# Hybrid decoder trunk on one core: parameters and memory weights of the S5 stage loaded inside the mixer, in shared on-chip rooms

## What is computed

```python
def s5_mixer(u, A_re, A_im, B_re, B_im, C_re, C_im, log_step, D, w_glu, b_glu):
    ug = u.reshape(b, L, 16, 16); delta = exp(log_step)[:, None]
    mag, ang = exp(A_re * delta), A_im * delta
    lr, li = mag * cos(ang), mag * sin(ang)
    ...                       # Bb = (B_re, B_im) scaled by (lambda - 1) / A
    xr, xi = scan(x[t] = lambda * x[t-1] + Bb @ ug[t])       # complex, 64 states
    y = C_re @ xr - C_im @ xi + D * u
    g = gelu(y)
    return g * sigmoid(g @ w_glu + b_glu)

def reference(x, mem, ...):
    mn = rmsnorm(mem, mem_norm_g)
    hn = rmsnorm(x, norm_mix_g)
    q, k, v, g, z, xbc, dt, u = split(hn @ w_in)
    h = x + concat(retention(q, k, v) gated by g, ssd(z, xbc, dt), s5_mixer(u)) @ w_out
    hn = rmsnorm(h, norm_cross_g)                            # 4 heads of 256
    h = h + softmax((hn @ w_cq) (mn @ w_ck)^T / 16) (mn @ w_cv) @ w_co
    h = h + hier_moe(rmsnorm(h, norm_ffn_g))                 # top 2 of 8 experts in 1 of 4 groups
    return rmsnorm(h, norm_final_g)
```

## Time and profile before

| | us |
|---|---|
| median of 3 runs | 2595.21 |
| lowest, highest | 2592.27, 2596.45 |
| the profiled execution's own time | 2593.17 |
| its span, first to last instruction | 2591.3 |

### The profile page before, as it was taken

How to read it: one execution, slowest core, us unless ns; L and a number is a source line. 1 busy time by engine, 2 the same in 40 slices (tenths; PEclk the granted TensorE clock), 3 DMA queues, 4 the chain that set the end, 5 groups by cost and what they waited for, 6 DMA issues and landing times. The chain is left out here.

```text
span 2591.3 us, 34611 instructions
## 1 busy us (share of the span) xinstructions
PE 2309.0 (89%) x12015; PEld 1308.7 (51%) x12016; DVE 1400.4 (54%) x2029; ACT 981.1 (38%) x1421; POOL 339.3 (13%) x277
## 2 busy tenths in 40 slices
PE   4999999999919988999999998179999999999980
PEld 2465565655618973555555554134444444444440
DVE  5566555664628843333333332757557677757823
ACT  4522533323211332222212221146446577657723
POOL 0022121220220000000000000002221222122212
PEclk8999999999959999999999999589999999999995
DMA  5201001010060133110111001369779999999927
GB/s 187 86 25 58 1 25 58 1 49 1 9 221 25 50 123 124 49 65 34 65 66 60 31 33 49 129 239 346 253 250 302 308 321 342 338 317 328 341 66 283
DMA packets 151797, 366.52 MB, mean 141 GB/s; under 512 B 24720, under 2 KB 30736, under 8 KB 151440
## 3 DMA queue, kind: packets, MB, share of 16 engines
q1 hardware_dynamic: 133120, 305.28, 32.3%
q0 software_dynamic: 13824, 50.34, 8.0%
q10 hardware_dynamic: 4752, 9.51, 1.0%
HBM read 303.75 MB, written 61.34 MB: 141 GB/s over the span
## 5 line engine op out<-in xcount | busy, mean ns | idle before, releaser
L110 PE MATMUL bankA<-wi,hnT 128*128 128x512 f16 (+1 forms) x1536 | 303.3, 356 | 5.5 <-DVE wi L498 5.5
L110 PE MATMUL bankE<-wg,xT 128*128 128x512 f16 x1152 | 262.2, 385 | 25.7 <-DVE xT L2432 21.5
L110 PE MATMUL bankE<-wu,xT 128*128 128x512 f16 x1152 | 259.0, 382 | 0.0
L110 PE MATMUL bankE<-wd,hT 128*128 128x512 f16 x1152 | 256.5, 379 | 1.7 <-DVE hT L2437 1.7
L110 PEld LDWEIGHTS bankA<-wi,hnT 128*128 128x128 f16 x1536 | 151.7, 99 | 148.8 <-issue 7.4
L110 PEld LDWEIGHTS bankE<-wg,xT 128*128 128x128 f16 x1152 | 113.9, 99 | 166.1 <-issue 34.3
L110 PEld LDWEIGHTS bankE<-wd,hT 128*128 128x128 f16 x1152 | 112.6, 98 | 137.6 <-issue 1.9
L110 PE MATMUL bankA<-hnT,wi 128*128 128x512 f16 x768 | 172.3, 387 | 9.0 <-DVE hnT L474 9.0
L110 PEld LDWEIGHTS bankE<-wu,xT 128*128 128x128 f16 x1152 | 113.3, 98 | 127.4 <-issue 3.3
L110 PE MATMUL bankC<-w_probs,probsT 128*128 128x512 f16 x768 | 172.0, 381 | 0.0
L110 PE MATMUL bankC<-score_w,hnT_c 128*128 128x512 f16 x768 | 170.7, 379 | 0.0
(11 more groups left out here) (400 smaller groups left out, 3402.1 us busy)
## 6 DMA issues: line engine op xcount, KB each, us to landing
w_rows<-in_w_gate SPq DMA_DIRECT2D x64, 1024.0 KB
w_rows<-in_w_up SPq DMA_DIRECT2D x64, 1024.0 KB
w_rows<-in_w_down SPq DMA_DIRECT2D x64, 1024.0 KB
xg<-in_x SPq DMA_DIRECT2D x4, 2048.0 KB, 10.9
cat_t<-scratch_cat SPq DMA_DIRECT2D x16, 512.0 KB, 4.9
Hc<-in_x SPq DMA_DIRECT2D x16, 512.0 KB, 5.6
scratch_ybuf<-Hc SPq DMA_DIRECT2D x16, 512.0 KB, 2.6
hf<-scratch_ybuf SPq DMA_DIRECT2D x16, 512.0 KB, 11.8
```

Of the source, the lines that this page charges most:

```text
L110: ins = pe.matmul(o, a[x][k], b[y][k], start=start and k == 0 and j == 0, stop=stop and k == n - 1 and j == 2)
```

## The change

Two buffers are now made at the start and shared by the stages. `main_room` holds `w_in` in the mixer. Behind it, its parts hold the work buffer of S5, `w_ck` (and later the score weights), the S5 result, the memory rows, half of `w_cv`, and in the cross stage the rows of h. `x_room` holds the tokens of a group in the mixer, and then all S5 parameters and small work tiles. A class `Rooms` cuts them up, and a class `Begun` issues the loads that now belong to the mixer:

```diff
+class Begun:
+    def params(self, sp):
+        dram = self.dram
+        sp.dma_start(self.step, dram["s5_log_step"][0].partition_broadcast(P)).then_inc(self.p_ld, 16)
+        sp.dma_start(self.ident, dram["cst"][:, K_ID:K_ID + P]).then_inc(self.p_ld, 16)
...
+        sp.dma_start(self.nhalf, dram["cst"][:, K_HALF:K_HALF + 2]).then_inc(self.gain_ld, 16)
+        sp.dma_start(self.mem_gain, dram["mem_norm_g"].rearrange("(k p) -> p k", p=P)).then_inc(self.gain_ld, 16)
+        sp.dma_start(self.cross_gain, dram["norm_cross_g"][0].rearrange("(k p) -> p k", p=P)).then_inc(self.gain_ld, 16)
+    def memory(self, sp):
+        sp.dma_start(self.rooms.mem, self.dram["mem"][0].rearrange("(m p) d -> p m d", p=P)).then_inc(self.mem_ld, 16)
+        rows = self.dram["w_ck"][0].rearrange("(k p) n -> p k n", p=P)
+        for h in range(2):
+            hh = slice(4 * h, 4 * h + 4)
+            sp.dma_start(self.rooms.w_ck[:, hh, :], rows[:, hh, :]).then_inc(self.k_ld, 16)
+    def values(self, sp):
+        rows = self.dram["w_cv"][0].rearrange("(k p) n -> p k n", p=P)
+        for h in range(2):
+            sp.dma_start(self.rooms.w_cv[h], rows[:, 4 * h:4 * h + 4, :]).then_inc(self.v_ld, 16)
...
 # mixer_projections, SyncE, behind the loop over the first three groups
-            stores(NG - 1, NG - 1)
+            sp.wait_ge(big, (NG - 1) * BIG + KT)
+            begun.params(sp)
+            sp.wait_ge(taken, NG * BIG - 2)
+            sp.dma_start(uv[NG - 1], dtu[:, :, SH:]).then_inc(u_st, 16)
+            sp.wait_ge(big, NG * BIG)
+            begun.memory(sp)
+            sp.wait_ge(out_done, NG * GC)
+            sp.dma_start(catv[NG - 1][:, :, 0:RW + SW], Y[:, :, :]).then_inc(cat_st, 16)
+            begun.values(sp)
             sp.wait_ge(u_st, 16 * NG)
             sp.wait_ge(cat_st, 16 * NG)
...
 # Memory
     def norm(self, pool):
-        pool.wait_ge(self.ld, 80)
+        pool.wait_ge(self.begun.gain_ld, 48)
...
-        pool.wait_ge(self.rsd, 1)
-        for m in range(MT):
-            pool.tensor_scalar(self.mem[:, m, :], self.mem[:, m, :], self.rs[:, m:m + 1], None, ALU.mult).then_inc(self.xs, 1)
...
+    def scale(self, act):
+        act.wait_ge(self.rsd, 1)
+        for m in range(MT):
+            act.activation(self.mem[:, m, :], self.mem[:, m, :], ACT.Copy, scale=self.rs[:, m:m + 1]).then_inc(self.xs, 1)
...
 # s5_mixer, SyncE, at the end
-            sp.dma_start(room[:, 0:2 * D].rearrange("p (k n) -> p k n", k=2), dram["w_co"][0].rearrange("(k p) n -> p k n", p=P)[:, 0:2, :]).then_inc(w_co_ld[0], 16)
+            for h, to in enumerate((big[:, 0:2 * D].rearrange("p (k n) -> p k n", k=2), rooms.mem)):
+                sp.dma_start(to, dram["w_co"][0].rearrange("(k p) n -> p k n", p=P)[:, 2 * h:2 * h + 2, :]).then_inc(begun.w_co_ld[h], 16)
...
 # s5_mixer, ScalarE
-            memory.loads(act)
-            memory.weight_loads(act)
             memory.squares(act)
+            memory.scale(act)
             act.wait_ge(ld, 16 * 14)
...
 # cross_and_router, SyncE
             sp.dma_start(ident[:, :], dram["cst"][:, K_ID:K_ID + P]).then_inc(ld, 16)
-            head(1)
             cat_in(0)
```

More of the change, by code:

```diff
@@ L126, in wait, with __init__, small @@
         self.eng.wait_ge(self.sem, self.turn * self.per + k if self.per else k)
-def mixer_projections(nc, env, dram):
+class Rooms:
+    def __init__(self, main, x_room):
+        m = main[:, :]
+        self.w_in = m.bitcast(F16).rearrange("p (h k n) -> p h k n", h=2, k=KT)
+        self.work = m[:, 0:8 * D]
+        self.score_w = m[:, 8 * D:16 * D].bitcast(F16).rearrange("p (h k n) -> p h k n", h=2, k=KT)
+        self.w_ck = m[:, 8 * D:16 * D].rearrange("p (k n) -> p k n", k=KT)
+        self.rows = m[:, 16 * D:22 * D].rearrange("p (i d) -> p i d", i=6)
+        self.y5, self.mem = m[:, 16 * D:20 * D], self.rows[:, 4:, :]
+        self.w_cv = [t.rearrange("p (k n) -> p k n", k=4) for t in (self.y5, m[:, 4 * D:8 * D])]
+        self.xg = x_room[:, :].rearrange("p (c d) -> p c d", c=GC)
+        self.free, self.at = x_room, 0
+    def small(self, rows, *shape):
+        n = int(np.prod(shape))
+        v = self.free[0:rows, self.at:self.at + n]
+        self.at += n
+        letters = "abcd"[:len(shape)]
+        return v.rearrange(f"p ({' '.join(letters)}) -> p {' '.join(letters)}", **dict(zip(letters, shape)))
@@ L909, in __init__ @@
         self.all_done = 3 * (KT // 2)
[L911 to L925, removed]
     def query_loads(self, sp):
@@ L1049, in sem @@
             return used[-1]
[L1051 to L1059, removed]
+        ident, anat, cnat, bnat, step = begun.ident, begun.anat, begun.cnat, begun.bnat, begun.step
+        d_bc, b_bc, wglu = begun.d_bc, begun.b_bc, begun.w_glu
+        w = rooms.small(P, 16, S5G)
         pw = sb("powers", [P, 2, SBL + 1, S5G])
         pv = sb("powers_back", [P, 2, SBL, S5G])
-        Ba, Bb, Bt = (sb(n, [P, S5G, S5C]) for n in ("Ba", "Bb", "Bt"))
-        Ca, Cb, Cc, Cd = (sb(n, [P, S5G, S5C]) for n in ("Ca", "Cb", "Cc", "Cd"))
+        Ba, Bb, Bt = (rooms.small(P, S5G, S5C) for n in range(3))
+        Ca, Cb = (rooms.small(P, S5G, S5C) for n in range(2))
+        Cc, Cd = (sb(n, [P, S5G, S5C]) for n in ("Cc", "Cd"))
         Cr, Ci = sb("Cr", [P, S5G, S5C]), sb("Ci", [P, S5G, S5C])
@@ L1068, in s5_mixer @@
         U = sb("U5", [P, 2, SBL, S5W])
-        Y5 = sb("Y5", [P, 2, SBL, S5W])
-        big = room[:, :]
+        Y5 = rooms.y5.rearrange("p (h s c) -> p h s c", h=2, s=SBL)
+        big = rooms.work
         tmp = [big[:, i * 2048:(i + 1) * 2048].rearrange("p (g b) -> p g b", g=S5G) for i in range(2)]
@@ L1524, with cross_and_router @@
 NCR, NHR, NXR = 3, 6, 3
[L1527 removed]
+def cross_and_router(nc, env, dram, score_w, values_t, logits, held, rooms, begun):
     with ExitStack() as ctx:
@@ L1534, in cross_and_router @@
         sem = nc.alloc_semaphore
+        room, hd_ld, wo_ld = rooms.work, begun.w_co_ld, begun.w_out_ld
         NR = NGR + NE
@@ L1540, in cross_and_router @@
         C = [sb(f"cat_t{i}", [P, D]) for i in range(NCR)]
-        HH = sb("Hc", [P, NHR, D])
+        HH = rooms.rows
         H = [HH[:, i, :] for i in range(NHR)]
```

94 lines of the change are left out of this document (47 added, 47 removed).

## The result

| | median us | lowest to highest | runs |
|---|---|---|---|
| before | 2593.82 | 2592.27 to 2596.45 | 4 |
| changed | 2570.67 | 2566.54 to 2573.14 | 4 |

The ratio is 0.9908, with a 95% interval of 0.9894 to 0.9922. The kernel is 23.15 us faster; the interval is a gain of 20 to 27 us. The profiled execution of the changed kernel took 2573.14 us, with a span of 2571.3; before, the span was 2591.3.

What follows compares the result with a forecast made beforehand. The prediction took late DMA landings, about 33 us after the barrier, as the bound. Chains -24.2 and barrier +0.3 gave -23.9 us: 2569.3 from the profiled 2593.17, 2571 as a median with 2.04 added; range 2565 to 2580.

Steps and rivals of the forecast that it cites:

- Both chains: S5 start: VectorE's parameter setup and TensorE's memory-row products, meeting within 0.3 us; each to start 24.2 us earlier.
- The cat store: Barrier at the mixer's end: w_cv queued behind the last cat store delays its landing, cost 0.3 us.
- the store of h: Cross stage: a 512 KB store with loads queued behind it, landing in 2.6 us; nearest row for the barrier's cost.
- The addition of 1.8 us: Barrier: skill-based estimate that the cat store lands 1.8 us later with w_cv behind it, about 2573 us in total.
- Rival (b): Barrier waits for all of w_cv, sharing engines with the store: 10.5 us added, gain 13.7, about 2581 us; chance 0.07.
- The scaling on ScalarE: S5 start: scaling the two memory rows moves from GpSimd, 5.68 us, to ScalarE, twice 1.06 us.
- The clock: TensorE's second clock fall at S5's memory products: taken as 0, bounds 1.7 us gained or lost.
- Rival (d): Gain of 27 us or more, 2568 or less, as the clock's second fall disappears and later stages fall well; chance 0.04.
- Rival (e): TensorE stays at the 1.2 GHz level through S5's 57 us memory chain: 33 us slower than before, 2628; chance 0.02.
- the prediction's signs of being wrong: Barrier moved by over 3 us, w_ck products below a clock of 0.9, or a later stage lengthened.

Runs made afterwards that it cites:

- three edits: Changed kernel with the memory rows' norm moved into the mixer, w_cv issued behind the barrier and the last cat store cut in two: 2556.81 us, ratio 0.9858.
- the last kernel: Kernel of three edits with GpSimd's norm of the memory rows moved ahead of the last chunk's scaling of Y: 2557.66 us, ratio 0.9866.

## Why the prediction was right

**Right, and shown.** The forecast was 2571 and the median is 2570.67. The mechanism held: the forecast gain was 23.9 us, and the median gain is 23.15. That the total agrees to 0.3 us is partly luck, as the median before, with one run more, is 1.4 us lower than the one it was counted from. The bound was the landing of the small loads: put back, they take 12.7 of 23.3 us. Their issue in the mixer costs nothing (14.1 us in front of 84 idle ones), nor do memory rows and w_ck. TensorE's and VectorE's waits for DMAs gave way to the ones named: GpSimd's clears and memsets, then ScalarE's scaling. Moving the norm past them gave 8.3 us at the products. Both chains gained alike, 24.0 for the products' start (771.65 to 747.64, forecast 24.2) and 24.02 for TensorE at the join. VectorE's setup starts at 742.03, 23.46 earlier; 24.1 had been forecast, and the missing 0.6 is the later barrier (732.26, where 731.65 had been put).

**The cat store, under-sized.** The step took +0.3 from the store of h; the barrier moved by 1.06, and 1.02 of it comes and goes with w_cv. The store of h was the wrong neighbour, as it moves 512 KB: the last part of the cut store, 384 KB, landed in 2.8 us with w_cv behind it and in 2.3 without, whereas with w_cv behind the 1.5 MB store S5 began at 6.95 to 6.97 in all six traces, against 5.90 to 5.95 in four traces without it. The Trainium skill (DMA: Bandwidth & Descriptors, "Latency and other measured facts") gives 0.2 us on average and 2 us at high load for HBM access. The addition of 1.8 us that the prediction estimated from it erred by as much on the other side, and the 384 KB store shows still less of it. The one trace that does not fit is that of the small loads alone: nothing behind the store, and yet 6.0 us to land and 6.51 to S5. Rival (b), a wait for all of w_cv, fell: 1 us and not 10.

**The scaling on ScalarE.** It was put at 2.1 us and took 2.19, in place of 5.68 on GpSimd. The trace with it back on GpSimd gives it a price of 2.97 us at the cross stage.

**The clock.** The zero was right for the change: both kernels have one second fall, 0.59 in four us here and 0.57 in the earlier trace rows. Rival (d) asked for its absence, and the kernel with w_cv behind the barrier shows that this exists and is worth 1.7 us before the join; there VectorE's chain comes last, so a further gain must come from both, as the prediction had said of its own gain. Rival (e), a memory chain at half clock, did not come.

**Where 3.7 us went.** The profiled execution gained 23.74 us up to the cross stage and 20.0 over the span. The loss can be laid out by stage, from one stage's first load to the next's (us):

| kernel | cross | route | experts and finish |
|---|---|---|---|
| before | 654.85 | 31.49 | 939.33 |
| before, again | 654.80 | 31.49 | 939.93 |
| changed | 656.97 | 32.13 | 940.31 |
| changed, again | 657.17 | 32.06 | 936.81 |

So two parts of the 3.7 us come back in the repeat: 2.1 to 2.4 in the cross stage and 0.6 in `route`, in both traces of the changed kernel and in neither of the kernel before. Only the last column varies with nothing changed, by 3.5 us, and it hides them in the total (1629.4 and 1626.0). This was one of the prediction's signs of being wrong, that a later stage lengthened: the cross stage was not "otherwise the same".

In the cross stage TensorE has 3072 products in all four traces, and 1.5 us are lost where the granted clock is lower. The same 50 us of work, the kernel before and then the changed one (columns as in the earlier trace rows):

```profile
1020.00:1070.00 50.00, 47.71 (x219) 24.47 (x220) 16.01 (x30) 12.73 (x32) 1.69 (x3) 0.97 0.11 42
```

```profile
996.30:1046.30 50.00, 48.09 (x214) 24.29 (x215) 15.98 (x29) 12.38 (x31) 1.48 (x3) 0.93 0.11 41
```

The granted clock in stretches of 10 us, counted from the cross stage's first load:

| kernel | 50 to 60 us | 60 to 70 us | cross stage |
|---|---|---|---|
| before | 0.83 | 1.00 | 654.85 |
| before, again | 0.83 | 1.00 | 654.80 |
| changed | 0.77 | 0.89 | 656.97 |
| changed, again | 0.78 | 0.88 | 657.17 |
| small loads alone | 0.76 | 0.90 | 656.75 |
| three edits | 0.74 | 0.91 | 656.49 |

The other eight traces have 0.83 and 1.00 there, and 654.72 to 655.20 us for the stage. Among them are kernels that issue all the loads in the mixer as the changed one does (scaling on GpSimd, norm ahead of the clears, norm in the mixer), so it is not those transfers as such; what makes the clock differ is open, and so is the 0.6 us in `route`. From the last cat store to the first load of the experts stage, both pairs of traces gain 20.5 us; the medians' 23.15 has an interval that reaches from 20 to 27.

## What to carry to other kernels

Ask of a hole between stages which loads land last, and count the small ones before the bytes: moving the twenty small loads alone gained as much as moving everything, and moving only the 9.5 MB gained less than half. Whether it is their packets or the time to issue them, 14.1 us even in an idle stretch, no run here separates; one with the same bytes in fewer loads would. What follows a barrier is a list in series (store's landing, clears, norm, scaling), and each edit brings up the next item, on another engine at times. To see what a change does to stages that it does not touch, trace both kernels twice and compare stage by stage: a total of 1626 us moved by 3.4 with nothing changed, and hid 2.7 that repeat. Below about three microseconds, read the granted clock of the stretch behind each edit before believing or dismissing a gain: here it took back 1 to 3 us from three edits that did start the work sooner.

## What the runs showed of the hardware

**VectorE held by a memset on GpSimd.** With the norm ahead of the clears, two scalings by a scalar of 128x16 took 2.41 us and not 0.39, ending with GpSimd's clearing of CZ. With the scaling on GpSimd, the same kind of instruction stood in the same way (the first row below, to 736.25, with GpSimd's clearing of CZ over 734.40 to 736.23), and the instructions with two inputs were only slowed, 14 of them taking 5.28 us instead of 4.42 beside GpSimd's scaling:

```profile
734.28 1.97 DVE L1199 TENSOR_SCALAR x_room<-x_room 128x16 f32<-128x16 f32 x2
...
739.42 5.28 DVE L1199 TENSOR_TENSOR x_room<-x_room 128x16 f32<-128x16 f32 x14
```

The Trainium skill (GPSIMD Engine Reference, "1. Specifications") says that GpSimd shares its SBUF interfaces with VectorE and that VectorE's instructions in a two-port mode or with two SBUF inputs contend with it. These traces agree in that both kinds of instruction took longer, though no view shows the mode in which one ran: the scalings by a scalar were held to the end of a GpSimd instruction of 1.84 us, and those with two inputs were only slowed, beside GpSimd's scaling. Beside a clearing of CZ they were not slowed at all (in the kernel of three edits five took 1.01 us from 731.92, with the clearing over 731.84 to 733.64; in the changed kernel, with GpSimd idle, 1.02).

**TensorE's granted clock differs from kernel to kernel, repeatably.** The same 256 products and what lies between them take 56.21 us in three traces, 57.7 to 58.0 in seven and 58.6 to 59.2 in four, and repeats of one kernel agree to 0.01 us. In the last kernel the products started 1 us sooner and took 3.0 longer. The three slow stretches come and go one by one: the one behind the join is absent with the big loads alone (134.67 us from join to cross) and there in the kernel of three edits (136.38), whose products had no second fall, and the one 50 to 70 us into the cross stage is there in four of fourteen traces, of three kernels. What decides them was not found.
